# Key tiles of the memory moved in between the experts, the router by token halves with an fp32 gather, and one expert tile loaded ahead

## What is computed

```python
# first block, behind its two mixers (mod = silu(c) @ w_ada + b_ada, split in sh1, sc1, g1, sh2, sc2, g2)
y = concatenate([attn, hm]) @ w_out                 # 1024 x 1024
x = x + g1 * y
h2 = rms_norm(x, norm2_g) * (1 + sc2) + sh2
# hier_moe: the best of 4 groups, in it the best 2 of 8 experts, for each token
logits = h2 @ [w_rg, w_re] + [b_rg, b_re]           # 4 + 32 columns
out[token] += weight * ((silu(h2 @ w1[e]) * (h2 @ w3[e])) @ w2[e])     # 32 experts, w1, w3: 1024 x 512, w2: 512 x 1024
x = x + g2 * out
# each later layer: keys and values of the memory
k, v = split(mem_n @ w_kv, 2)                       # 1024 x 2048
```

## Time and profile before

| | |
|---|---|
| median of 3 runs | 1497.86 us (1497.14 to 1498.14) |
| span of the profiled execution | 1498.7 us |
| TensorE busy | 1344.3 us, 90% |
| VectorE, ScalarE, GpSimd busy | 660.6, 264.8, 228.2 us |
| DMA, mean over the span | 259 GB/s, 387.69 MB |

### The profile page before, as it was taken

The page is one execution under the profiler, slowest core; times in us unless marked ns, Lnnn a source line. Parts: engine busy times, 40 slices in busy tenths (PEclk is TensorE's granted clock), DMA queues, the critical chain, the costliest instruction groups (busy, mean ns, idle before and its releaser), DMA issues. The chain is left out here.

```text
span 1498.7 us, 25139 instructions
## 1 busy us (share of the span) xinstructions
PE 1344.3 (90%) x10377; PEld 1002.5 (67%) x10377; DVE 660.6 (44%) x1236; ACT 264.8 (18%) x557; POOL 228.2 (15%) x223
## 2 busy tenths in 40 slices
PE   5999988977687777767899999999999998999998
PEld 2475746644444455444568788888887887788887
DVE  2544335111111011101354327376299999986563
ACT  2213202110010001100211022010233333330000
POOL 0000000000000000000166550099322122000000
PEclk9999998999988789988999999999999999999999
DMA  9635775999999999999843343556564444334440
GB/s 399 240 146 225 282 306 201 410 429 429 426 429 429 426 430 429 428 429 428 337 177 124 112 163 118 196 182 223 181 218 142 156 166 141 145 112 167 155 174 39
DMA packets 49930, 387.69 MB, mean 259 GB/s; under 512 B 6192, under 2 KB 21296, under 8 KB 27968
## 3 DMA queue, kind: packets, MB, share of 16 engines
q1 hardware_dynamic: 47264, 381.35, 64.2%
q10 hardware_dynamic: 2592, 5.31, 0.9%
HBM read 379.76 MB, written 6.88 MB: 258 GB/s over the span
## 5 line engine op out<-in xcount | busy, mean ns | idle before, releaser
L2478 PE MATMUL ps<-hT,ring 128*128 128x256 f32 x768 | 171.9, 384 | 1.0 <-PEq L1918 1.0
L2478 PEld LDWEIGHTS ps<-hT,ring 128*128 128x128 f32 x768 | 146.9, 193 | 21.3 <-issue 1.4
L1391 DVE TENSOR_TENSOR act_slots<-gate,ps 64x256 f32<-64x256 f32 x32 | 13.5, 423 | 303.8 <-ACT gate L1339 303.8
L1288 PE MATMUL ps<-expert,x_gathered 128*32 128x256 f32 x1024 | 83.5, 484 | 62.9 <-DMA expert<-in_experts 61.8
L1288 PEld LDWEIGHTS ps<-expert,x_gathered 128*32 128x32 f32 x1024 | 36.9, 134 | 106.9 <-DMA expert<-in_experts 77.0
L1458 POOL TENSOR_SCALAR end_stat<-end_ss 128x1 f32<-128x1 f32 x2 | 0.9, 472 | 507.5 <-ACT expert L1448 507.4
L266 PE MATMUL ps<-ring,hT 128*128 128x512 f32 x160 | 69.8, 593 | 0.0
L1288 PE MATMUL ps<-ring,x_gathered 128*32 128x256 f32 x1024 | 61.0, 389 | 8.9 <-DMA ring<-in_experts 8.9
L1767 PE MATMUL ps<-ring,zT 128*128 128x256 f32 x288 | 66.8, 379 | 0.0
L1270 PE MATMUL ps<-mem_quarter,memT 128*128 128x128 f32 x256 | 43.7, 350 | 21.7 <-DMA mem_quarter<-in_mem_quarters 21.7
L1368 DVE TENSOR_SCALAR sel_weighted<-const,rank,comb 128x128 f32<-128x128 f32 x66 | 19.9, 344 | 93.0 <-PE ps L1249 91.5
(11 more groups left out here) (651 smaller groups left out, 2542.9 us busy)
## 6 DMA issues: line engine op xcount, KB each, us to landing
ring<-in_weights SPq DMA_DIRECT2D x71, 2048.0 KB, 8.1
expert<-in_experts SPq DMA_DIRECT2D x48, 2048.0 KB, 26.5
ring<-in_experts SPq DMA_DIRECT2D x48, 2048.0 KB, 27.1
mem_quarter<-in_mem_quarters SPq DMA_DIRECT2D x12, 512.0 KB, 20.6
s_c_bar<-c_bar_out ACTq DMA_DIRECT2D x16, 256.0 KB, 2.3
c_bar<-s_c_bar SPq DMA_DIRECT2D x16, 256.0 KB, 2.6
mem_tile<-in_weights SPq DMA_DIRECT2D x1, 2048.0 KB, 18.1
b_raw<-in_s_b SPq DMA_DIRECT2D x16, 128.0 KB, 7.1
```

What stands on the lines that cost most here:

```text
L1288: last = pe.matmul(h_ps[group(g), :], xg[:, f, group(b)], w[:, kk, g, :], start=(f == 0), stop=(f == KD - 1))
L1391: dve.tensor_tensor(act_s[:], gate[:], h_ps[w3_out, :], ALU.mult).then_inc(act_ready, 1)
L2478: last = pe.matmul(out[:, f, :], w[:, kk, (2 * h + f) * P:(2 * h + f + 1) * P], k.hT[:, kk, :], start=(kk == 0), stop=(kk == KD - 1))
```

## The change

- M0 and M1 leave `FRONT` and TensorE's programs of the mix and router stages. Their 8 quarter tiles stand in `mem_quarters` ahead of the 12 others, and are multiplied between the experts: in pairs 0 to 3 a quarter follows the odd expert's first products beside the piece of M2; in pairs 4 to 7 there are two quarters a pair; pairs 8 to 15 have one, as before. The results go to `kmT` and `kept`. Two of the 20 quarters are loaded in the router stage. The piece has a half bank of its own (bank 7), beside `y`'s.
- One more expert tile, the first of expert 2, is loaded into a buffer of its own right behind the tile VM (`load_early`). The slot that it would have had takes expert 4's first tile one pair earlier.
- The end of the mix stage and the router stage go by token halves: squares, scale, turn and modulation of the first 128 tokens begin before the output product of the second 128 is done. A10 moves into the mix stage. The router's product has its 36 columns as weights, and is turned afterwards.
- The tokens for the gather are held in fp32 (`tokens`), 16 products a pair in place of 48; the split into three parts is gone.
- The last pieces' order: inter-chunk products, column product of A7, then A8. The denominators are made ahead of the copy of `mixT`. The first three tiles of the next layers are issued in another order. `dynamic_dma_scratch_size=1024` makes room in SBUF.

The core of the diff (left out: names of semaphores and buffers, the rest of the router's reordering, the host's arrays):

```diff
-FRONT = ("A0", "A2", "A1", "A3", "Q", "K", "V", "U0", "A4", "U1", "A5", "VM", "OM", "A6", "A7", "M0", "A8", "A9",
-         "O0", "O1", "A10", "M1", "A11", "M2")
+FRONT = ("A0", "A2", "A1", "A3", "Q", "K", "V", "U0", "A4", "U1", "A5", "VM", "OM", "A6", "A7", "A8", "A9",
+         "O0", "O1", "A10", "A11", "M2")
...
-                for n in range(7, TILE_OF["M1"] + 1):
+                for n in range(7, TILE_OF["A11"] + 1):
                     tile(n)
-                    if n == 14:
+                    if n == TILE_OF["VM"]:
+                        load_early(k, sp, a)
+                    if n == TILE_OF["A7"]:
                         load_expert(k, sp, a, 0, 0)
-                    if n == 17:
+                    if n == TILE_OF["A9"]:
...
-                half("M00", "fm", k.memT)
-                ada_columns(k, banks, pe, 7, part)
...
-                half("M01", "fm", k.memT)
                 pe.wait_ge(c_out, 1)
                 for h in range(4):
                     last = pe.matmul(quarter(4, h), qT(h, 1), cst[:, h, :], start=True, stop=True)
                 last.then_inc(inter_done, 1)
+                ada_columns(k, banks, pe, 7, part)
                 ada_tile(k, banks, pe, 8, crep)
...
+                for t in range(TT):
+                    for n in range(N_OUT):
+                        out_half(1, t, n).then_inc(k.tile_done if t else o_part, 1)
+                turn_x(0)
+                ada_tile(k, banks, pe, 10, crep)
+                ada_row(k, banks, pe, 10, part)
+                turn_x(1)
...
+                add_out(0, 0)
+                add_out(0, 1)
+                add_out(1, 0)
+                scale_x(0)
+                add_out(1, 1)
+                dve.wait_ge(x1_turned, 1)
+                dve_modulate(k, a, dve, 0).then_inc(h_first_ready, 1)
+                scale_x(1)
+                take_row(10, k.row("b_g2")[:, 0:512])
...
-                tile(TILE_OF["A11"])
+                load_expert(k, sp, a, 1, TILE_OF["O1"] % RING)
+                load_expert(k, sp, a, 1, TILE_OF["A10"] % RING)
+                for b in range(2):
+                    load_part(k, sp, a, b, N_KEYS0 // 2 * (1 - b))
+                sp.wait_ge(k.tile_done, TILE_OF["A11"] + 1)
+                load_expert(k, sp, a, 1, TILE_OF["A11"] % RING)
...
+def load_part(k, sp, a, b, i):
+
+    sp.dma_start(a["parts_w"][b][:].rearrange("p k n -> p (k n)"),
+                 k.dram["mem_quarters"][i] if isinstance(i, int) else
+                 k.dram["mem_quarters"][bass.ds(i, 1)].rearrange("a p n -> (a p) n")).then_inc(a["parts_in"][b], 16)
+
+
+def load_early(k, sp, a):
+
+    sp.dma_start(a["early"][:], k.dram["experts"][3 * EARLY]).then_inc(a["early_landed"], 16)
...
+                def logits_of(t):
+                    for kk in range(KD):
+                        last = pe.matmul(by_expert_ps[:, t * P:(t + 1) * P], w_router[:, kk, :], k.hT[:, kk, t * P:(t + 1) * P],
+                                         start=(kk == 0), stop=(kk == KD - 1))
+                    return last
+
+                def turn_back(t):
+                    for f in range(KD):
+                        last = pe.transpose(a["turned_x"](t)[:, f, :], k.hT[:, f, t * P:(t + 1) * P], k.c("ident"))
+                    last.then_inc(h_turned, 1)
+
                 pe.wait_ge(router_in, 32)
-                for t in range(TT):
-                    for kk in range(KD):
-                        last = pe.matmul(k.ps[:, 4 + t, 0:36], k.hT[:, kk, t * P:(t + 1) * P], w_router[:, kk, :],
-                                         start=(kk == 0), stop=(kk == KD - 1))
-                last.then_inc(logits, 1)
-                ada_row(k, banks, pe, 10, a["part"])
-                for t in range(TT):
-                    for f in range(KD):
-                        last = pe.transpose(k.ps[:, 2 * t + f // 4, (f % 4) * P:(f % 4 + 1) * P],
-                                            k.hT[:, f, t * P:(t + 1) * P], k.c("ident"))
-                last.then_inc(h_turned, 1)
-                half_tile(k, banks, pe, "M11", "fm", k.memT)
+                logits_of(0)
+                pe.wait_ge(h_ready, 2)
+                logits_of(1).then_inc(logits, 1)
+                turn_back(0)
+                pe.wait_ge(logits_copied, 1)
+                for t in range(TT):
+                    last = pe.transpose(logits_ps[:, 36 * t:36 * t + 36], by_expert[:, t * P:(t + 1) * P], k.c("ident")[0:36, 0:36])
+                last.then_inc(logits_turned, 1)
+                turn_back(1)
...
+        SEGMENTS = ((0, 1, ("first", "keys0")), (1, 1, ("first", "keys0")), (2, 2, ("first", "keys0")), (4, 4, ("keys0", "keys1")),
+                    (8, 8, ("values", None)))
...
+                def load_pair(p, i, off, next_parts):
 
                     for b in range(2):
+                        js = range(1, 3) if off == 1 and b == 0 else range(3)
                         load(b, p * N_EXP + i * 2 + (2 * off + b),
-                             lambda j: k.dram["experts"][bass.ds(i * 6 + (6 * off + 3 * (b + 2) + j), 1)]
-                             .rearrange("a p n -> (a p) n"))
-                        if part and b == 0:
-                            sp.wait_ge(part_taken, p * N_PAIR + i + (off + 1))
-                            sp.dma_start(part_w[:].rearrange("p k n -> p (k n)"),
-                                         k.dram["mem_quarters"][bass.ds(i + (off - 3), 1)].rearrange("a p n -> (a p) n")
-                                         ).then_inc(part_in, 16)
+                             lambda j: k.dram["experts"][bass.ds(i * 6 + (6 * off + 3 * (b + 2) + j
+                                                                          + (6 if off == b == j == 0 else 0)), 1)]
+                             .rearrange("a p n -> (a p) n"), js)
+                        if next_parts[b] is not None:
+                            sp.wait_ge(part_done[b], p * (N_SECOND if b else N_PAIR) + i + (off + 1))
+                            load_part(k, sp, a, b, i + (off + 1 + next_parts[b]))
...
-                            for part in range(3):
-                                last = pe.matmul(xg_ps[:, f, :], a["h2"][:, t, part, f * P:(f + 1) * P],
-                                                 sel[:, t].rearrange("p e s -> p (e s)"),
-                                                 start=(t == 0 and part == 0), stop=(t == TT - 1 and part == 2))
+                            last = pe.matmul(xg_ps[:, f, :], a["tokens"][:, t, f * P:(f + 1) * P],
+                                             sel[:, t].rearrange("p e s -> p (e s)"), start=(t == 0), stop=(t == TT - 1))
...
                         for j in range(2):
-                            pe.wait_ge(landed[b][j], n_landed)
-                            w = rings[b][j].rearrange("p (k g n) -> p k g n", k=4, g=4)
+                            if off == 1 and b == j == 0:
+                                pe.wait_ge(a["early_landed"], p * 16 + 16)
+                                w = a["early"][:]
+                            else:
+                                pe.wait_ge(landed[b][j], n_landed_first if b == j == 0 else n_landed)
+                                w = rings[b][j]
...
-                        if b == 0:
-                            memory_part(p, i, off, part)
+                        if parts[b] is not None:
+                            pe.wait_ge(y_ready, s + 1)
+                            memory_part(p, i, off, b, parts[b])
```

340 lines of the change are left out of this document (179 added, 161 removed).

## The result

The change made the kernel slower: 1507.12 us median (1506.37 to 1507.86) against 1498.0 us for the kernel before on the same chip, ratio 1.0045, 95% interval 1.0025 to 1.0066. The forecast was 1485.5, range 1478 to 1494. The profiled execution has a span of 1506.1 us; before it was 1498.7.

The account below looks back on a forecast made before the run. The prediction took TensorE to bound the time ahead of the first refill and the DMA queue the experts' stage behind it. Its terms, -18.6 + 3.7 + 2.3 = -12.6 us, gave a median of 1485.5 us, range 1478 to 1494.

Parts of the forecast that it names:

- Step 3: Router stage: bias wait, low-clock logits at 228.4, choice at 233.9, VectorE done at 236.6, gather at 239.4 after a 1.5 us turn.
- Steps 1 and 2: Mix stage without the key products: first half of the output product starts at 177.8, 12.7 us earlier; stage ends at 215.4.
- Step 2: End of the mix stage: second half ends at 208.8, then turns and A10; stage ends at about 215.4, before 223.2.
- Step 4: Gather in fp32: 16 products take 3.8 us, bounds 1.57 to 5.5; first expert at 245.5 against 264.1, 18.6 us earlier.
- low-clock rival: Low clock stays for the gather, first pair and tail: 6 us less gain, 1491 us; chance 1 in 6.
- Step 5: Bytes behind the first refill in the experts' stage: 93.5 tiles against 92.75 at 4.89 us each, +3.7 us.
- Step 6: TensorE in the expert pairs: 25.3 us of work against 30.6 us of queue per pair, hidden; a short hole costs nothing.
- slower rival: TensorE becomes the bound in pairs 0 to 7: up to 34 us slower than forecast, 1519 us; chance 1 in 18.
- Step 7: Tail behind the last quarter tile, with one gather in it: +2.3 us; all later stages shift unchanged.

Follow-up runs that it names:

- e1: Changed kernel with norm_f's load issued ahead of the wait for A11 and the third expert tile; ratio 1.0013 to the kernel before.
- e3: Kernel before with norm_f's load moved last in the routing block, behind three expert tiles and the key quarter; ratio 1.0120.
- e8: Changed kernel with norm_f, O0 and bias loaded earlier, seven semaphores left out of the clearing between layers, TensorE's routing-block waits filled with unread products; ratio 0.9960.
- e2: e1 with O0 issued ahead of the second tile of expert 0; ratio 0.9988 to the kernel before.
- e14: e11 with one more filling product at the routing block's end and four between the zeroing and the gather; ratio 0.9951 to the kernel before.
- e9: e2 with the router's bias loaded behind O1, and expert 2's first tile loaded with the refills instead of early; ratio 0.9995 to the kernel before.
- e12: Changed kernel with seven of eight products left out of each key quarter multiplied between the experts, all loads kept; ratio 1.0019 to the kernel before.
- e4: Kernel before with the scratch for dynamic transfers set to 1024, as in the changed kernel; ratio 1.0004.
- e7: Kernel before with seven more idle semaphores, cleared between the layers with the others; ratio 0.9993.
- e11: e2 with the bias behind O1, norm_f ahead of all the routing block's expert tiles, and seven unread products filling TensorE's waits there; ratio 0.9954 to the kernel before.
- e10: e11 with seven semaphores left out of the clearing between the layers; ratio 0.9957 to the kernel before.

## Why the prediction was wrong, point by point

The profiled execution ends 20.0 us later than the forecast (+7.4 for -12.6). By the steps:

| step | forecast | measured | us |
|---|---|---|---|
| 1, 2: mix stage ends | 215.4 | 221.36 | +6.0 |
| 3: from there to VectorE's last step | 21.2 | 21.1 | 0 |
| 3: from there to the gather | 2.8 | 6.7 | +3.9 |
| 4: gather | 3.8 | 7.09 | +3.3 |
| 4, 5: gather's end to first refill | 4.5 | 4.7 | +0.2 |
| 5: first refill to last quarter | 447.9 | 450.4 | +2.5 |
| 7: last quarter to last scatter | 20.5 | 20.5 | 0 |
| 7: "all later stages shift as they are" | 770.0 | 774.3 | +4.3 |

(The sum is 20.2, the rounding apart. Last row: from the last scatter's start to the end.)

- **Step 3 failed in one sentence**, "To the first selection 1.5 us of turning the stage". SP's queue in the diff puts norm_f behind the third expert tile, and that behind A11; the block waits for it. Before, it was issued at 224.5, ahead of the block's expert tiles; the order of loads in the diff shows the move, and I did not price it. Shown by e1, e3 and by SP's wait in e8. Worth 3.5 us at the turn (e1); the ratios differ by 4.8 us (1.0045 to 1.0013), but were taken apart from each other, and with the bias landing sooner in e1's profile.
- **Steps 1 and 2**: the half began at 181.45, not 177.8, and took 16.42, not 14.0. Of the 6.0 us, 1.7 are the front, whose issues are as much late (158.02 for 156.34 in the earlier trace rows): TensorE's first tile landed 0.6 later and a modulation tile at 26.68 took 3.23 us for 1.92 at a lower clock, long before the early tile is issued at 109.8; 1.9 are O0's landing, for which I had taken the time at which the queue's windows run empty, not that at which the last tile is signalled; 2.4 are the low clock after that wait. e2 gave 2.9 back. The faults are O0's landing time and a wait of TensorE's costed at its length alone. (Step 2's parts add up to 215.2, not 215.4, and step 3's are rounded up by another 0.3; that changes nothing.)
- **Step 4**: the price at full clock was right, 3.68 us in e14 and in the stage's middle for the 3.8 taken. Behind the logits I let the low clock cost 1.2 us in all; it cost 3.3 at the gather and 2.1 in the first products. The upper bound of 5.5 for the gather was wrong too: it came from a row of which only a part ran at 0.50, and 7.09 is the price. The low-clock rival was nearer here, but had its gathers at the same 5.5. e14 shows that the clock, and not the product, makes the difference. The FP8 and Floating Point Precision page of the Trainium skill (TensorE Precision Notes) has four passes for fp32; by streamed columns that was 2.1 us, and the 3.68 of e14 disagree. (By that count the forecast would have been 3.5 us faster, 1.7 at the first gather and 1.8 in the tail, and not 1.8 in all as I wrote.)
- **Step 5**: the tile's price held (e9). The stretch took 2.5 us more. In the 40 us from the first refill on, the queue moves 399 GB/s against 415 before, which is 1.5 of them. Only 0.6 can be the low clock, since in e14, whose first pair ran at full clock, the stretch is 449.8. The rest stays open. Small loads cost little rate: from 20 us behind the first refill to the last quarter it is 426 to 429 GB/s, before 427 to 429.
- **Step 6 was right** about TensorE, but for the short hole that it cost at nothing, where the rate above falls. Two successive pairs are 25.2 us apart in SP's issues (311.54 to 336.72, forecast 25.3), and e12 shows that TensorE's key products do not set the stage's length. The slower rival that I named was wrong. Slower had a chance of 0.07 and came mostly by waits that I had not listed.
- **Step 7**: the tail was right. "All later stages are the same code and shift as they are" failed: they took 4.3 us more, of which 0.4 are the longer wait ahead of the second layer, 1.7 its first tile and 1.9 the products behind the scan, both at a lower clock. e4 excludes the scratch, e7 and e8 the number of semaphores; what makes the clock dip there is open.

Of the gain forecast, a part is there to be had: with norm_f, O0 and the bias put where they bind less and TensorE's waits filled, e14 runs at 0.9951, 7 us below the kernel before, where the forecast was 0.9917.

## What to carry to other kernels

When work is taken out ahead of a bound, list every load that it covered and every load whose place in the queue the diff changes, small ones too, with the wait that needs it. Here that is O0, an 18 KB bias, and a load of 512 KB that had slid behind two waits and held the turn for 3.5 us. Put such small loads first in the queue. And price a wait of TensorE as its length plus a range for slower products behind it: 2.4 us behind 4.55 here, 6.2 behind 1.19 and 0.80 (e11), nothing behind 2.61 in the kernel before. To price work at the low clock, take a row whose whole length is at that clock.

## What the hardware showed unexpectedly

- Two short waits were enough to lose the clock, and the same waits did not always cost the same. 1.19 and 0.80 us ahead of the gather took it from 1.00 to 0.50 for some 13 us (e11); in e10, with waits of 1.18 and 0.81, it fell later, and the gather took 6.38 us for 7.08. With four products in place of the second wait and one more ahead of the first it stayed up (e14). In the profile of before, a wait of 2.61 us left it at 1.00, and in e7, the same code but for idle semaphores, it fell behind the same wait and the first products took 6.41 us for 3.66. The page TensorE: Matmul & The Clock Gate of the Trainium skill (HAM oscillation) tells of a loop whose bursts of about 2 us between waits of 3 to 5 us for DMA run cold every time; here shorter waits were enough in e11, and in the kernel before 2.61 us were not.
- Taking work from TensorE where a queue binds lowered its clock from 0.96 to 0.83 and left it nearly as busy, 158 us of 180 for 163 (e12).
- Unchanged code of 750 us came out up to 3.9 us longer, and the front of 220 us, the same code in e10 and e11, moved by 3.7 us between two executions; differences of that size between two profiles are no evidence for an edit.
